# Even and odd expert slots summed in separate PSUM bank pairs, the last two slots of a layer one at a time, and one query weight load moved into the pause between the layers

## The reference

```python
def one(hb):                                  # 128 tokens
    q = (hb @ w_q).reshape(128, 8, 2, 64)     # 8 heads
    s = jnp.einsum('thpk,hpnk->thpn', q, sub_keys)
    ...                                       # top 16 of 16384 experts per token and head -> idx, sc
    gate = jax.nn.softmax(sc, axis=-1)
    act = gelu(jnp.einsum('td,thkd->thk', hb, u_tab[idx]))
    return jnp.einsum('thk,thkd->td', gate * act, v_tab[idx])
...
x = x + mod_x[5][:, None, :] * peer(hx2, p_w_q[i], p_keys[i], p_u[i], p_v[i])
```

## Time and profile before

| | |
|---|---|
| median of 3 runs | 2523.17 us (2519.55 to 2525.32) |
| the profiled execution | 2522.06 us, of which the span is 2520.2 us |
| TensorE busy | 1779.5 us, 71% |
| VectorE busy | 1640.0 us, 65% |
| ScalarE busy | 970.2 us, 38% |
| GpSimd busy | 978.6 us, 39% |
| DMA | 938.58 MB, mean 372 GB/s; gathers 807.34 MB of it |
| the chain that ended last | DMA 40%, TensorE 33%, VectorE 10% |

### The profile page before, as it was taken

How to read it: one execution, slowest core, us unless ns; L and a number is a source line. 1 busy time by engine, 2 the same in 40 slices (tenths; PEclk the granted TensorE clock), 3 DMA queues, 4 the chain that set the end, 5 groups by cost and what they waited for, 6 DMA issues and landing times.

```text
span 2520.2 us, 35252 instructions
## 1 busy us (share of the span) xinstructions
PE 1779.5 (71%) x13118; PEld 848.4 (34%) x13118; DVE 1640.0 (65%) x3836; ACT 970.2 (38%) x2654; POOL 978.6 (39%) x896
## 2 busy tenths in 40 slices
PE   7998889897875868556665566766987655656554
PEld 5877566544542224112221122221544211111111
DVE  1544457878997675677766776764377666666665
ACT  3411147553433333335433353542334333333333
POOL 3014123344443443355444444442034445444442
PEclk9999989998988879678887788987998878687877
DMA  8268669999999999999999999998279999999997
GB/s 345 77 274 342 264 244 373 403 421 395 369 363 422 420 422 377 417 421 421 421 421 418 415 419 421 412 398 352 101 299 420 421 421 421 414 414 421 416 417 287
DMA packets 127821, 938.58 MB, mean 372 GB/s; under 512 B 17153, under 2 KB 18177, under 8 KB 20641
## 3 DMA queue, kind: packets, MB, share of 16 engines
q0 software_dynamic: 114800, 807.34, 78.2%
q1 hardware_dynamic: 12848, 128.97, 12.7%
HBM read 935.10 MB, written 1.15 MB: 371 GB/s over the span
## 4 chain that ended last, share of the span: by engine, by line
DMA 40%; PE 33%; DVE 10%; issue 6%; ACT 6%; POOL 4%; SPq 0%; POOLq 0%; DVEq 0%; ACTq 0%
DMA arena<-in_experts,expert_cur 39%; PE ps L2024 12%; PE ps L1217 11%; POOL arena L1930 4%; DVE arena L2106 4%; ACT diag L1950 2%; PE ps L1229 2%; PE ps L1766 2%; PE ps L1242 2%; ACT coef L1946 1%; PE ps L1442 1%; DMA arena<-in_w_mod 1%; PE ps L1423 1%; ACT acts L1945 1%; DVE straight L1984 1%
## 5 line engine op out<-in xcount | busy, mean ns | idle before, releaser
L2024 PE MATMUL ps<-arena,diag 64*64 64x512 f32 x6144 | 989.2, 772 | 639.1 <-ACT diag L1950 636.3
L1930 POOL DMA_INDIRECT arena<-in_experts,expert_cur x768 | 909.7, 1185 | 1281.8 <-PE ps L2024 985.2
L2106 DVE CUSTOM_DVE_ANT_0 arena<-arena 128x1024 f32<-128x1024 f32 x768 | 942.9, 1228 | 572.9 <-DMA arena<-in_experts,expert_cur 564.3
L2024 PEld LDWEIGHTS ps<-arena,diag 64*64 64x64 f32 x6144 | 241.0, 160 | 1288.1 <-ACT diag L1950 935.9
L1945 ACT ACTIVATE acts<-dots 128x2 f32<-128x2 f32 x384 | 78.2, 204 | 1029.7 <-DVE dots L2106 1029.1
L1950 ACT ACTIVATE diag<-consts,coef 128x128 f32<-128x128 f32 x768 | 266.1, 393 | 12.5
L1946 ACT ACTIVATE coef<-acts,gate_cur 128x1 f32<-128x1 f32 x768 | 184.9, 288 | 12.6
L1217 PE MATMUL ps<-wring 128*128 128x256 f32 (+2 forms) x568 | 144.7, 406 | 0.7 <-DVE wring L2706 0.7
L1217 PE MATMUL ps<-arena,wring 128*128 128x256 f32 (+1 forms) x576 | 118.8, 366 | 6.4 <-issue 5.6
L1217 PEld LDWEIGHTS ps<-wring 128*128 128x128 f32 x568 | 99.2, 193 | 62.7 <-issue 53.9
L1217 PEld LDWEIGHTS ps<-arena,wring 128*128 128x128 f32 x576 | 102.6, 202 | 24.6 <-issue 12.4
(11 more groups left out here) (378 smaller groups left out, 1822.1 us busy)
## 6 DMA issues: line engine op xcount, KB each, us to landing
wring<-in_w_mod SPq DMA_DIRECT2D x18, 2048.0 KB, 10.0
wring<-in_ev_w_in SPq DMA_DIRECT2D x14, 1024.0 KB, 9.6
arena<-in_w_mod SPq DMA_DIRECT2D x6, 2048.0 KB, 10.4
wring<-in_ev_w_in SPq DMA_DIRECT2D x6, 2048.0 KB, 14.1
arena<-in_experts,expert_cur POOLq DMA_INDIRECT x768, 12.2
wring<-in_w_q SPq DMA_DIRECT2D x5, 2048.0 KB, 11.7
wring<-in_ev_w_out SPq DMA_DIRECT2D x3, 2048.0 KB, 12.5
wring<-in_od_w_out SPq DMA_DIRECT2D x2, 2048.0 KB, 8.2
```

Of the source, the lines that this page charges most:

```text
L1930: nc.gpsimd.indirect_dma_start(ring[:, k % RING, :], None, table, bass.IndirectOffsetOnAxis(ap=expert_cur[:, par, k:k + 1], axis=0),).then ...
L2024: last = nc.tensor.matmul(ps[rows_of(o), sum_bank(G // PH, i, c), :], diag[rows_of(i), slot, rows_of(i)], ring[rows_of(i), slot, D + 512 * ...
L2106: ins = nc.vector.tensor_tensor_reduce(out=ring[:, slot, 0:D], in0=ring[:, slot, 0:D], in1=place, scale=1.0, scalar=0.0, op0=ALU.mult, op1 ...
```

## The change

Five edits:

1. The bank pair is chosen by the slot's parity. Even slots go straight into banks +0 and +1 on all 128 rows, odd slots crossed into banks +2 and +3.
2. Tiles 0, 1, 2 and 4: ScalarE copies the crossed sum as before, now from one bank pair. VectorE adds the straight sum from PSUM into the place in one instruction of 128x1024, without the two copies.
3. In the last head of T = 3 and T = 5 the slots 14 and 15 are handled singly by ScalarE and TensorE (8 matmul instructions each), and both go straight, so that the crossed sum is complete after slot 13.
4. For these two tiles ScalarE copies nothing. VectorE multiplies the crossed halves by the gate row out of PSUM (two of 64x1024) and adds them to `x` once slots 12 and 13 are summed; when slot 15 is summed it multiplies the straight sum (one of 128x1024) and adds it to `x`.
5. `q1_1` goes into `x`'s two context tiles and is issued behind `keys1` in the pause, after `("st", 1)`; the wait for `("sc", 15)` and the issue behind it go away.

```diff
--- before.py
+++ after.py
@@ -462,7 +462,7 @@
         w_uq_n, w_uq_r, w_ukv_3 = wring[:, 2560:5632], wring[:, 5632:7168], area(0, 4096)
         w_uq_n3, w_uq_r3 = area(7040, 3072), area(10112, 1536)
         w_out1 = [wring[:, 4096 * c:4096 * c + 4096] for c in range(2)]
-        w_q1 = [wring[:, 8192:10240], area(16384, 2048), wring[:, 0:4096]]
+        w_q1 = [wring[:, 8192:10240], x[:, 0:2, :].rearrange("p t d -> p (t d)"), wring[:, 0:4096]]
         krT, lat_gain = late[:, 0:512], late[:, 512:1152]
         rope_cs = late[:, 1152:1280].rearrange("p (t i a n) -> p t i a n", t=2, i=2, a=2)
         ktmp = late[:, 1280:1408].rearrange("p (i n) -> p i n", i=4)
@@ -630,7 +630,7 @@
         gexp_ready = sem("gate_exp_ready")
         peer_crossed = sem("peer_crossed_halves_copied")
         peer_straight = sem("peer_straight_halves_copied")
-        gated = Order(sem("gated_sum_ready"), [(0, t) for t in range(NTOK)] + [(1, t) for t in (2, 3)])
+        gated = Order(sem("gated_sum_ready"), [(0, 0), (0, 1), (0, 2), (1, 2)])
         N_EARLY, N_SECOND_EARLY = GROUPS.index(("mcol",)), GROUPS.index(("ht", "m1", 2, 0))
@@ -1906,15 +1906,37 @@
-        GROUPS_OF_HEAD = TOPK // GRP
-        def sum_bank(T_, i, c):
-            return (0 if T_ in (2, 5) else NBANK_SUMS) + 2 * i + c
-        def sum_of(T_, i, o):
-            return ps[rows_of(o), sum_bank(T_, i, 0):sum_bank(T_, i, 0) + 2, :]
+        PAIRS = [(k, k + 1) for k in range(0, TOPK, GRP)]
+        LAST_TILES = (3, 5)
+        SINGLES_FROM = 14
+        TAIL_GROUPS = PAIRS[:SINGLES_FROM // GRP] + [(k,) for k in range(SINGLES_FROM, TOPK)]
+        def ends_alone(G):
+            return G % PH == PH - 1 and G // PH in LAST_TILES
+        def groups_of(G):
+            return TAIL_GROUPS if ends_alone(G) else PAIRS
+        def groups_before(G):
+            return sum(len(groups_of(g)) for g in range(G))
+        def sum_bank(T_, odd, c):
+            return (0 if T_ in (2, 5) else NBANK_SUMS) + 2 * odd + c
+        def straight_sum(T_):
+            return ps[:, sum_bank(T_, 0, 0):sum_bank(T_, 0, 0) + 2, :]
+        def crossed_sum(T_, i):
+            return ps[rows_of(1 - i), sum_bank(T_, 1, 0):sum_bank(T_, 1, 0) + 2, :]
+        def by_banks(rows):
+            return rows.rearrange("p (a b) -> p a b", a=2)
         KEYS_SLOT = 12288 // (2 * D)
         LATE_SLOT = 10240 // (2 * D)
@@ -1940,13 +1962,14 @@
         def sums_act(act, G, par, j):
-            g = slice(j * GRP, (j + 1) * GRP)
-            act.wait_ge(dots_ready, G * GROUPS_OF_HEAD + j + 1)
+            ks = groups_of(G)[j]
+            g = slice(ks[0], ks[-1] + 1)
+            act.wait_ge(dots_ready, groups_before(G) + j + 1)
             act_step(nc.scalar.activation(acts[:, par, g], dots[:, par, g], ACT.Gelu))
             act_step(*[nc.scalar.activation(coef[:, par, k:k + 1], acts[:, par, k:k + 1], ACT.Copy,
                                             scale=gate_cur[:, par, k:k + 1])
-                       for k in range(j * GRP, (j + 1) * GRP)])
-            for k in range(j * GRP, (j + 1) * GRP):
+                       for k in ks])
+            for k in ks:
                 nc.scalar.activation(diag[:, k % RING, :], const(IDENT), ACT.Copy,
                                      scale=coef[:, par, k:k + 1]).then_inc(diag_ready, 1)
@@ -1959,7 +1982,7 @@
         def head_act(act, G, par, rank_next, between=lambda: None):
             act.wait_ge(ranked, G + 1)
-            for j in range(GROUPS_OF_HEAD):
+            for j in range(len(groups_of(G))):
                 if j in STAGE_AT:
                     between()
                 sums_act(act, G, par, j)
@@ -1972,20 +1995,45 @@
         def tile_sum_act(act, T_, place):
+            if T_ in LAST_TILES:
+                return
             tile_summed(act, T_)
             for i in range(2):
-                nc.scalar.copy(place.rearrange("p (a b) -> p a b", a=2)[rows_of(i)], sum_of(T_, i, 1 - i)).then_inc(
-                    peer_crossed, 1)
+                nc.scalar.copy(by_banks(place)[rows_of(i)], crossed_sum(T_, i)).then_inc(peer_crossed, 1)
         def tile_sum_dve(dve, T_, place):
             tile_summed(dve, T_)
+            dve.wait_ge(peer_crossed, 2 * T_ + 2)
+            nc.vector.tensor_tensor(by_banks(place), by_banks(place), straight_sum(T_), ALU.add).then_inc(peer_straight, 1)
+            dve.wait_ge(peer_straight, T_ + 1)
+        def last_gate(T_):
+            return peer_gate1 if T_ == 5 else peer_gate[:, 1, :]
+        def crossed_residual_dve(dve, T_, t):
+            dve.wait_ge(bc_landed[f"pg{T_ // 5}",], 16 if T_ == 5 else 32)
+            dve.wait_ge(slot_free, (T_ + 1) * SLOTS - TOPK + SINGLES_FROM + RING)
+            if T_ == 3:
+                dve.wait_ge(product.sem, product.count(("o", HC // 2 - 1)))
+            else:
+                dve.wait_ge(product.sem, product.count(("q1", 3, 3)))
             for i in range(2):
-                nc.vector.tensor_copy(straight.rearrange("p (a b) -> p a b", a=2)[rows_of(i)], sum_of(T_, i, i)).then_inc(
-                    peer_straight, 1)
-            dve.wait_ge(peer_straight, 2 * T_ + 2)
+                nc.vector.tensor_tensor(by_banks(straight[:, :])[rows_of(i)], crossed_sum(T_, i),
+                                        by_banks(last_gate(T_))[rows_of(1 - i)], ALU.mult).then_inc(peer_crossed, 1)
             dve.wait_ge(peer_crossed, 2 * T_ + 2)
-            dve_step(nc.vector.tensor_tensor(place, place, straight[:, :], ALU.add))
+            dve_step(nc.vector.tensor_tensor(x[:, t, :], x[:, t, :], straight[:, :], ALU.add))
+        def straight_residual_dve(dve, T_, t):
+            tile_summed(dve, T_)
+            nc.vector.tensor_tensor(by_banks(straight[:, :]), straight_sum(T_), by_banks(last_gate(T_)), ALU.mult).then_inc(
+                peer_straight, 1)
+            dve.wait_ge(peer_straight, T_ + 1)
+            x_ready.mark(nc.vector.tensor_tensor(x[:, t, :], x[:, t, :], straight[:, :], ALU.add), (f"p{T_ // 5}", t))
         def tile_open_pe(pe, T_):
@@ -2007,25 +2055,26 @@
         def sums_copied(pe, T_):
             pe.wait_ge(peer_crossed, 2 * T_ + 2)
-            pe.wait_ge(peer_straight, 2 * T_ + 2)
+            pe.wait_ge(peer_straight, T_ + 1)
         def head_pe(pe, G, between=lambda: None):
-            for j in range(GROUPS_OF_HEAD):
+            for j, ks in enumerate(groups_of(G)):
                 if j in STAGE_AT:
                     between()
                 opens = j == 0 and G % PH == 0
                 if opens:
                     tile_open_pe(pe, G // PH)
-                pe.wait_ge(diag_ready, G * TOPK + GRP * j + GRP)
+                pe.wait_ge(diag_ready, G * TOPK + ks[-1] + 1)
                 for c in range(2):
                     for i in range(2):
-                        for s in range(GRP):
-                            slot, o = (GRP * j + s) % RING, (i + s) % 2
-                            last = nc.tensor.matmul(ps[rows_of(o), sum_bank(G // PH, i, c), :],
+                        for k in ks:
+                            slot, odd = k % RING, k % 2 if len(ks) == 2 else 0
+                            o = (i + odd) % 2
+                            last = nc.tensor.matmul(ps[rows_of(o), sum_bank(G // PH, odd, c), :],
                                                     diag[rows_of(i), slot, rows_of(i)],
                                                     ring[rows_of(i), slot, D + 512 * c:D + 512 * c + 512],
                                                     start=opens, stop=True, skip_group_check=True)
-                last.then_inc(slot_free, GRP)
+                last.then_inc(slot_free, len(ks))
         def scores_of(G):
@@ -2106,8 +2155,10 @@
                 ins = nc.vector.tensor_tensor_reduce(
                     out=ring[:, slot, 0:D], in0=ring[:, slot, 0:D], in1=place, scale=1.0, scalar=0.0,
                     op0=ALU.mult, op1=ALU.add, accum_out=dots[:, G % 2, k:k + 1])
+                alone = ends_alone(G) and k >= SINGLES_FROM
+                if alone or k % GRP == GRP - 1:
+                    ins.then_inc(dots_ready, 1)
                 if k % GRP == GRP - 1:
-                    ins.then_inc(dots_ready, 1)
                     between(k // GRP in STAGE_AT)
                 else:
                     between(False)
@@ -2131,7 +2182,9 @@
                 head_dve(dve, G, tile_place(T_), ranks.get(G + 1), ranks.get(G + 2), between,
                          (lambda: tile_sum_dve(dve, T_ - 1, tile_place(T_ - 1))) if T_ > first and G % PH == 0
                          else (lambda: None))
-            tile_sum_dve(dve, last, tile_place(last))
+            t = last if last < NTOK else last - 2
+            crossed_residual_dve(dve, last, t)
+            straight_residual_dve(dve, last, t)
         def tile_place(T_):
@@ -2610,7 +2663,6 @@
                         peer_residual_dve(dve, 0, 2)
                 heads_dve(dve, range(4 * PH), lambda starts: weaves[weave_at(head[0])](starts), at_head)
```

(7 more changed lines are left out.)

## The result

In the runs made side by side, 14 of each kernel, the changed kernel takes 2503.14 us (median; 2498.41 to 2512.61) and the kernel before 2519.45 (2513.2 to 2526.55): ratio 0.9936 [0.9925, 0.9947], 16.3 us less. Over all runs of this study, the profiled executions among them, the kernel before has a mean of 2518.9 (111 runs, standard deviation 4.8) and the changed kernel of 2504.35 (31 runs, 4.2). Their difference, 14.5 +- 1.8 us (two standard errors), is the best figure for the gain; 12.1 was forecast. The median of 2503.14 lies 1.9 us under the low end of the range that the prediction gave, 2505.

What follows compares the result with a forecast made beforehand. Bounds differ by stage: DMA in saturated gather stretches, dependent chains in the pause and at the end, a ring running dry. 4.5 + 2.5 + 3.4 + 1.2 + 0.5 = 12.1 us, taking 2523.17 to 2511.1; range 2505 to 2519.

Steps and rivals of the forecast that it cites:

- D: Rival: VectorE's lead at the tile ends pays in full, 14.9 us in all, giving 2508.3; chance 0.1.
- Step 1: Chain at the end of T = 3: x ready 4.8 us earlier, 4.5 after an allowance for keep_busy.
- Step 2: Load of q1_1 leaves the saturated gather stretch and hides under the attention in the pause: 2.5 us.
- Step 3: Chain at the end of T = 5: x, and the norm and store behind it, come 3.4 us earlier.
- Step 4: Ends of tiles 0, 1, 2 and 4: VectorE loses two copies; 1.2 us at T = 0, 0.5 at the others.
- Step 5: Banks of a pair: same quarters in the same order, still writing different banks where rows coincide; cost 0.
- A: Rival: both tails run at the half clock, Step 1 gives 0 and Step 3 0.5 us, 2518.5; chance 0.08.
- B: Rival: moving q1_1 gives nothing, as late-freed slots limit the start of layer 1; 2513.6; chance 0.12.
- C: Rival: row halves sharing a bank are served serially, a pair takes 3.7 instead of 1.95 us; 2564; chance 0.05.

Runs made afterwards that it cites:

- banks_only: Changed kernel with the q1_1 load at its old place and the tails of before, so banks by parity and direct addition remain: 2513.43 us, 0.9979 of the kernel before.
- experiment 4: The two runs on the banks alone, banks_only with the direct addition and banks_copies with copies: 0.9979 and 0.9991 of the kernel before.
- banks_copies: As banks_only, but the straight sum is again copied in two halves and then added, so only the bank choice is new: 2519.25 us, 0.9991.
- late_load: Changed kernel with the 1 MB q1_1 load back at its old place: 2506.38 us, 0.9943 of the kernel before.
- no_keep: Changed kernel without the four keep_busy matmuls that only keep TensorE busy ahead of the norm: 2505.82 us, 0.9946 of the kernel before.
- load_only: Kernel before with only the q1_1 load moved behind the keys: 2512.82 us, 0.998 of the kernel before.
- before_again: Kernel before, unchanged, run for a second profile: 2517.48 us, ratio 1.0.
- after_again: Changed kernel, unchanged, run for a second profile: 2507.84 us, 0.9954 of the kernel before.

## Why the prediction was right or wrong

**The step that failed is the base of the sum,** "the median 2523.17 to 2511.1", with the allowance for scatter at the low end. Behind it stands a gain that was sized too small. From 2511.1 to 2503.14 are 8.0 us: 4.3 because 2523.17, the median of three runs, stood that far above the mean of 111; 2.4 because the gain was 14.5 and not 12.1, mostly the part that no stage shows (below); 1.2 because the 14 runs of the first comparison lay below the mean of all 31. (In that comparison by itself the base is 3.7 of the 8.0 and the gain 4.2, 16.3 instead of 12.1; had either been as forecast, the time would have lain inside the range, at 2506.9 or 2507.4.) The profiled execution that I used as a second witness, 2522.06, was as high and not independent evidence of the level. With a standard deviation of 4.8, a median of three is uncertain by about 3 us, and 2518.9 - 12.1 = 2506.8 would have been inside the range. "D less some 3 of scatter" allowed for the runs of after and not for those of before.

**Step 1** (4.5 us) measured 4.1. Its inner working was right to a tenth in the profile on record: the crossed part at once behind the dot product, 2.47 + 1.23, slot 15 under it at 1.94, then 1.22 + 1.22, x after 6.28 against 6.3. The gain on x was 4.8 and part of it was lost to keep_busy where the clock fell in it, the loss that I put at 0.3 for a range up to 3.7; it was 1.5 in one profile of three. Some luck is in the 4.8: 1.3 of it is that the old pair ran at 3.24 in this profile and not at 1.95. In the four profiles of the old form that pair took 1.95 to 3.69 and x came 11.0 to 12.8 after the dot product's start; in the changed kernel's three it came 7.5 to 8.1 after it, as VectorE's crossed work covers a slow slot. A slot alone costs what a pair costs: 1.94 for its 8 instructions, which use two of the four quarters (1735.64 in the profile on record), and 1.95 for a pair's 16 (1737.22 in banks_only), both at a granted clock of 1.00.

**Step 2** (2.5) measured 1.5 to 1.8, within its bounds. I priced all of the load's bytes at the saturated rate. The stream is not saturated in its first 6 us (247 GB/s), and some of them fit there, the more so if the load is issued ahead of the gathers.

**Step 3** (3.4) measured 3.7, and 3.5 in the pair of profiles on record. The pair before the singles, which I took at 3.42, ran at full clock (granted clock 1.00 from 2486.60 to 2490.40); since VectorE came to the crossed part only at the dot product's end in either case, that was worth 0.1.

**Step 4** (1.2 at T = 0, 0.5 at the others) measured 2.1 and nothing, the 2.1 with the doubt of experiment 4. TensorE's part is 1.26 as forecast (2.57 - 1.31), and the windows give 1.3 and 2.2 us of bytes. The rest could be VectorE's lead, which is rival D for this one place, but no run shows that; at T = 1, 2 and 4 the lead pays nothing.

**Step 5** (0) holds: banks_copies is level with the kernel before.

**The rivals.** A is false as it was priced: the kernel is far below its 2518.5, and the singles ran at 1.93 to 1.94 in both tails of the profile on record. Its mechanism does occur: over the six profiles of the new tails slot 14 ran partly at the half clock in six of twelve tails, up to 3.20 in late_load (granted clock 0.50 there up to 2504), and x then came up to 1.3 us later (8.83 in no_keep against 7.52). B is false, since load_only is faster; the load gave 1.5 to 1.8 of its 2.5. C, a supposition for which the kernel before had no row, since each row half had its own bank there, is false: with two row halves that write different rows of one bank a pair takes 1.95 in banks_only and banks_copies, as before, and banks_copies is at a ratio of 0.9991 [0.9972, 1.001]. D, 2.5 at T = 0 and 2 at the others, is false for the others and open at T = 0.

**What stays open.** The stages account for 11.4 of 14.5 +- 1.8 us. I found no stage in the profiles that holds the remaining 3. The stretch ahead of T = 0's sum, whose TensorE and VectorE work is the same but for the banks, is 1.5 +- 4 us shorter, which may be chance. Banks_only has such a remainder already, so it may belong to the banks and the addition. TensorE's granted clock over the whole span is 0.856 in the mean of the changed kernel's 31 runs and 0.851 in 96 of the kernel before; it could hold a part, but no run isolates it, and banks_only gained its 5.2 at 0.850. Nor do the parts add up closely: load_only, banks_only and the singles (11.5) give 4.9 + 5.2 + 11.5 = 21.6 us by the means, where the whole is 14.5; each has an error of 2 to 3 us, and the 11.5 holds 2 us of keep_busy's push, which neither the kernel before nor, in two of three profiles, the changed one has.

## What to carry to other kernels

Ask of a chain's tail which operand could be complete one step sooner, and only then split the last piece of work: the halves by parity shortened no tail until the last two slots went singly, and then each by 3.5 us at the full clock. Ask as well what else on the path runs beside a step before you count the step as saved: two copies taken from VectorE gave 0.4 us, since ScalarE's copies beside them stayed. Measure what a half-sized piece costs: here a slot alone, on two of the four quarters, took 1.94 us and a whole pair 1.95, so the split was worth what it let another engine cover. And before a forecast of half a per cent, ask how far the median of the few runs given may lie from the kernel's level; it was about half of the error here.

## What the runs showed of the hardware

The granted clock fell to half for about 10 us in the middle of the pause in some executions and not in others of the same kernel (0.50 from 1770 to 1780 in before_again, 1.00 from 1779.17 to 1789.17 in the first profile of before, as far behind the transposes), while TensorE was busy all of the time (24 matmuls in 10.00 busy us in before_again, 40 in the same stretch at a granted clock of 1.00 in after_again); the pause was 4.6 us longer with it (90.43 against 85.85). A 64x1024 multiplication out of PSUM whose output goes to the other 64 rows took 1.22 to 1.23 us, as the copy of that shape did (1.21 to 1.23), and 128x1024 out of PSUM took 1.22: here twice the rows cost no more time, and one instruction over 128 rows did what two over 64 did in 2.47.
